# The factors of queries and keys in the second attention, as one power of minus a half on GpSimd

## The chip, the cores and the metric

The kernel runs on one core of a Trainium2 chip. The metric is the device time of one execution in microseconds (us); less is better.

## What is computed

Two transformer blocks in a row over 1024 positions of width 1024, in fp32. The change lies in the second block, in the preparation of queries and keys for its stick-breaking attention with eight heads of 64 columns:

```python
def rms_norm(x, g):
    return (x * lax.rsqrt(jnp.mean(x * x, axis=-1, keepdims=True) + EPS)) * g

q = rms_norm(q.reshape(bsz, s_len, ATTN_HEADS, HEAD_DIM), q_norm_g[i])
k = rms_norm(k.reshape(bsz, s_len, ATTN_HEADS, HEAD_DIM), k_norm_g[i])

def stick_breaking_attention(q, k, v):
    for qb in range(s_len // Q_BLOCK):
        z = einsum(qi, kj) * HEAD_DIM ** -0.5          # causal, s < t
        log_rem = where(causal, log_sigmoid(-z), 0.0)
        suffix = cumsum(log_rem, reverse=True) - log_rem
        weights = where(causal, exp(log_sigmoid(z) + suffix), 0.0)
        o = einsum(weights, vj)
```

The factor `rsqrt(mean + EPS)` of each head and position is what the change computes in another way.

## The kernel before

The program is written out engine by engine; each engine runs its own queue in the order of the code, and semaphores tie them. TensorE computes every projection as three matmuls for each tile of 128 rows (high part times high part, low part, and again), so each unit of weights (128x1024) has to be split into w_hi and w_lo. In the stretch of the change GpSimd does the splitting: `split` computes w_hi as w_raw plus a column of zeros and w_lo as w_raw minus w_hi, unit u starting when TensorE has finished both halves of unit u - 2.

The second attention works on pairs of heads; the code's `HEADS` is 4, and "head" below is such a pair, number p from 0 to 3. A head is cut into `NSEG` = 12 segments n: a block of 128 queries against up to 512 keys, 128, 256, 384 or 512 columns wide. Segments 0 to 4, 6, 8 and 10 end in the masked diagonal; 5, 7, 9 and 11 are the remaining 512 columns of the queries of the segment before. For each segment and each of the two heads in the pair (hh):

- TensorE: logits (line 1737) into a bank, and, one segment behind, the transposes of the weights (line 1747), then, two behind, the product with the values (line 1761). Between these, `norm_fill` and `fill` put matmuls of the projections that come next (lines 1199 to 1201; three units for a head: queries, keys, values).
- ScalarE (all its instructions have line 2829): `sb`, the sigmoid of minus z; `sa`, the sigmoid of z; `swt`, a copy of the transposed weights. In its queue of segment n the order is sb(n) twice, swt(n-1, 0), sa(n) twice, swt(n-1, 1).
- VectorE: `remains`, two scans (line 2681) over sb; `weights`, the mask on the diagonal (line 2692) and the product `sw` of sa and the scan (line 2697). At the end of a segment it moves finished projections out of their banks (line 1912).

While head p runs, the factors of head p + 1 are made. ScalarE squares its queries and keys (`square`), TensorE sums the squares (`head_sums`, line 1268) into a bank as a tile of 128x256, and then, on the tile hsm (128x256):

- VectorE, after the products of segment 6: `head_mean`, mean plus EPS, from the bank into hsm (line 1933), which raises `st_var`;
- ScalarE, after segment 7's queue: `head_sqrt`, the root in place, which raises `st_root`; the sigmoid and the root are in different tables, so a table load stands before and behind it;
- VectorE, after the products of segment 7: `head_factor`, the reciprocal in place (line 1938), which raises `st_inv`;
- SyncE's queue: `spread_qk_factors`, 16 rows of hsm to memory (line 970) and four transfers back that spread them over all partitions of `spread_qk` (line 976). Behind them in this queue stand the loads of the next units of weights (line 984);
- VectorE, at segment 10: scales queries and keys of the next head by the gain and by spread_qk (line 2731).

This happens for heads 1, 2 and 3 (`SPREAD_QK`). Head 0 uses the same functions through `head_inverse` and gets its factors by matmuls; so does a norm behind the attention.

Of the kernel before, what the change touches and what calls it, by code (L numbers as in the profile page):

```python
# [22 lines left out]
ALU = mybir.AluOpType  # L23
# [3 lines left out]
P = 128  # L27
T = 1024
# [6 lines left out]
HEADS = 4  # L35
# [18 lines left out]
DER = {}  # L54
_at = 0
for _name, _n in (("fin_n1", 8), ("subln", 1), ("qn", 1), ("neg_lam", 1), ("lb", 8), ("omlb", 8),
                  ("g0", 8), ("g1", 8), ("lamp", 2), ("lame", 2), ("zero", 1)):
    DER[_name] = _at
    _at += _n
NDER = _at  # L60
# [7 lines left out]
U_SB = U_PLE + KT  # L68
# [4 lines left out]
U_OUT2 = U_SU + 2  # L73
# [10 lines left out]
N_FIN = N_PLE + 1  # L84
N_1 = N_FIN + 1
N_QK = N_1 + 1
# [6 lines left out]


SPREAD_QK = tuple(range(N_QK + 1, N_QK + HEADS))


def bc_no(n):

    return n + 1 - len([m for m in SPREAD + SPREAD_QK if m <= n])  # L100

# [162 lines left out]
def half_no(u, hf):  # L264

    return 2 * u + hf + 1
# [35 lines left out]
def da_calm(u):  # L302
    h, n = divmod(u - U_DA - 6, 3)
    if h + 1 < HEADS:
        return KT * h + (3, 6, 8)[n], KT * h + (4, 7, 9)[n]
    return ((KT * h + 5, KT * h + 6), (KT * h + 8, KT * h + 8))[n]
# [45 lines left out]
S_SUM = 13  # L352


def bass_two_blocks(nc, io):
    ctx = ExitStack()
    with ctx:
        def at(name, cols, off, dt=F32, parts=P):
            shape = [parts, *cols] if isinstance(cols, tuple) else [parts, cols]
            return nc.alloc_sbuf_tensor_at(name, shape, dt, offset=SBUF_BASE + off)  # L360

        def sem(name):
            return ctx.enter_context(nc.semaphore(name))
# [24 lines left out]
        der = at("der", NDER, VEC_END)  # L388
# [85 lines left out]
        hsm = at("hsm", T // 4, S0 + 57 * KB)  # L474
# [113 lines left out]
        st_var = sem("st_var")  # L588
        st_root = sem("st_root")
        st_inv = sem("st_inv")  # L590
# [22 lines left out]
        der_ready = sem("der_ready")  # L613
# [378 lines left out]
        def _(pool):  # L992
            pool.memset(der[:, DER["zero"]:DER["zero"] + 1], 0.0).then_inc(der_ready, 1)
            pool.wait_ge(der_ready, 1)
            zero = der[:, DER["zero"]:DER["zero"] + 1]
            pool.memset(sinm[:, :], 0.0).then_inc(cs_clear, 1)
            pool.memset(cosm[:, :], 1.0).then_inc(cs_clear, 1)
            for m in range(2):
# [2 lines left out]
            def split(u0, n, cols=(T, T)):  # L1001
                def one_unit(u, s, turn, high_there, calm=None):
                    if not high_there:
                        if calm:
                            pool.wait_ge(w_ready, calm[0])
                        pool.wait_ge(w_in[s], 16 * (turn + 1))

                        pool.wait_ge(acc_full, half_no(u - 2, 1))
                        nc.gpsimd.tensor_tensor(w_hi[:, s, 0:cols[s]], w_raw[:, s, 0:cols[s]],  # L1009
                                                zero.to_broadcast([P, cols[s]]), ALU.add).then_inc(w_hi_done, 1)  # L1010
                    pool.wait_ge(w_hi_done, u + 1)
                    if calm:
                        pool.wait_ge(w_ready, calm[1])
                    nc.gpsimd.tensor_tensor(w_lo[:, s, 0:cols[s]], w_raw[:, s, 0:cols[s]],  # L1014
                                            w_hi[:, s, 0:cols[s]].bitcast(F32), ALU.subtract).then_inc(w_split, 1)

                if u0 == 0:
                    for s in range(2):
                        one_unit(s, s, 0, True)
                    with pool.Fori(1, n // 2, 1) as i:  # L1020
                        for s in range(2):
                            one_unit(2 * i + s, s, i, False)
                    for u in range(n, U_HG + 5):
                        one_unit(u, u % 2, u // 2, False, da_calm(u))
                else:
                    with pool.Fori(0, n // 2, 1) as i:
                        for s in range(2):
                            one_unit(u0 + 2 * i + s, s, u0 // 2 + i, False)
# [143 lines left out]
            split_ahead(U_SB + 2)  # L1172
            pool.wait_ge(st_inv, N_1 + 1)
            split_ahead(U_SB + 3)
            split(U_SB + 4, U_OUT2 - U_SB - 4)
            lows_and_sums(FF2, U_OUT2, T, Q_2)
            feed_forward(FF2, of2, U_PLE2)
            split(U_PLE2 + 2, KT - 2)
# [706 lines left out]
        def _(dve):  # L1885
# [5 lines left out]
            def step(ins):  # L1891

                ins.then_inc(dve_step, 1)
                steps[0] += 1
                dve.wait_ge(dve_step, steps[0])
# [38 lines left out]

            def head_factor(n):

                dve.wait_ge(st_root, n + 1)
                nc.vector.reciprocal(hsm[:, :], hsm[:, :]).then_inc(st_inv, 1)

            def head_inverse(n):  # L1940
# [3 lines left out]
            def row_inverse(n, scale):  # L1944

                dve.wait_ge(st_sum, n + 1)
                ts(rsm[:, :], ps[:, 7, 0:P], scale, EPS, ALU.mult, ALU.add).then_inc(st_var, 1)
                dve.wait_ge(st_root, n + 1)
                nc.vector.reciprocal(rsm[:, :], rsm[:, :]).then_inc(st_inv, 1)

            def da_guard(h):
# [224 lines left out]
            for h in range(HEADS):  # L2176
                u = U_HG + 5 * h
# [107 lines left out]
                for d in range(2):  # L2285

                    n = 2 * h + d
# [367 lines left out]
            dve.wait_ge(st_sum, N_1 + 1)  # L2655
            fin, both = hsm[:, 0:P], hsm[:, P:2 * P]
            ts(fin, ps[:, 7, 0:P], 1.0 / T, EPS, ALU.mult, ALU.add).then_inc(st_var, 1)
            dve.wait_ge(st_root, N_FIN + 1)
            nc.vector.reciprocal(fin, fin).then_inc(st_inv, 1)
            dve.wait_ge(st_inv, N_FIN + 1)  # L2660
            step(stt(both, ps[:, 7, P:2 * P], 1.0 / T, fin, ALU.mult, ALU.mult))
            step(tt(both, both, fin, ALU.mult))
            ts(both, both, EPS, None, ALU.add).then_inc(st_var, 1)
            dve.wait_ge(st_root, N_1 + 1)
            step(nc.vector.reciprocal(both, both))
            tt(both, both, fin, ALU.mult).then_inc(st_inv, 1)
            dve.wait_ge(rstd_ready, 4)
# [41 lines left out]
            for p in range(HEADS):  # L2709
                slots = sb_slots(p)  # L2710
                u_next = sb_fill(p)[0]
                if p + 1 < HEADS:
                    next_ = [sk[(p + 1) % 2][:, 0, :], sk[(p + 1) % 2][:, 1, :], sv[:, :]]
                else:
                    next_ = [cc[:, j, :] for j in range(3)]
                for n in range(NSEG + 1):
                    if n < NSEG:
                        remains(p, n, 0)
                        remains(p, n, 1)
                        weights(p, n, 0)  # L2720
                        weights(p, n, 1)
                    if p + 1 < HEADS:
                        if n == S_SUM // 2:
                            head_mean(N_QK + p + 1, 1)
                        elif n == S_SUM // 2 + 1:
                            head_factor(N_QK + p + 1)
                    evict(slots[2 * n] + slots[2 * n + 1], u_next, next_)
                    if p + 1 < HEADS and n == NSEG - 2:
                        dve.wait_ge(qk_fac_in, 64 * (p + 1))
                        for t, gain in enumerate((dcol("qn"), col("kn"))):  # L2730
                            stt(sk[(p + 1) % 2][:, t, :], sk[(p + 1) % 2][:, t, :], gain, spread_qk[:, t, :],
                                ALU.mult, ALU.mult).then_inc(qk2_ready, 1)
# [94 lines left out]
        def _(act):  # L2827
# [29 lines left out]
            def head_sqrt(n):  # L2857

                act.wait_ge(st_var, n + 1)
                av(hsm[:, :], hsm[:, :], ACT.Sqrt).then_inc(st_root, 1)  # L2860
# [146 lines left out]
            for h in range(HEADS):  # L3007
                u = U_HG + 5 * h
# [400 lines left out]
            for p in range(HEADS):  # L3409
                if p == 0:  # L3410
                    square(0, 0)
                    square(0, 1)
                    act.wait_ge(st_bc, bc_no(N_1))
                    av(rstd_f[:, :], banks(2), ACT.Copy).then_inc(xf_ready, 1)
                    head_sqrt(N_QK)
                    act.wait_ge(x_out, 16 * KT)
                for n in range(NSEG + 2):
                    if n < NSEG:
                        betas(p, n, 0, True)
                        betas(p, n, 1, True)  # L3420
                    if n == 6 and p + 1 < HEADS:
                        square(p + 1, 1)
                    if n == 0:
                        act.wait_ge(sv_tr, p + 1)
                        av(svt[:, :, :], banks(6).rearrange("p (c e) -> p c e", c=KT),
                           ACT.Copy).then_inc(sv_ready, 1)
                    if 1 <= n <= NSEG:
                        turned_weights(p, n - 1, 0)
                    if n < NSEG:
                        betas(p, n, 0, False)  # L3430
                        betas(p, n, 1, False)
                    if 1 <= n <= NSEG:
                        turned_weights(p, n - 1, 1)
                    if n >= 2:
                        out_rows(p, n - 2)
                    if p + 1 < HEADS:
                        if n == 4:
                            square(p + 1, 0)
                        elif n == 7:
                            head_sqrt(N_QK + p + 1)  # L3440


            act.wait_ge(so_out, 2 * HEADS)
# [164 lines left out]
```

## Time and profile before

| | us |
|---|---|
| median of 3 runs | 2714.21 |
| lowest, highest run | 2710.95, 2714.23 |
| the profiled execution | 2713.26 |
| its span | 2711.5 |

| engine | busy, us | share of the span |
|---|---|---|
| TensorE (PE) | 2653.9 | 98% |
| VectorE (DVE) | 1985.6 | 73% |
| GpSimd (POOL) | 1359.2 | 50% |
| ScalarE (ACT) | 1121.3 | 41% |

The granted clock of TensorE is 0.998 of full speed. Times in rows are microseconds from the start of the span. The second attention runs from about 1515 to 1795; the factors for head 1 are made between 1563 and 1585, those for heads 2 and 3 about 69 and 138 us later. In a timeline, x2 means two instructions in a row that were merged, and the bracket at the end tells how long the engine stood idle before the first and what released it. The ends of matmuls are modelled: one is shown with 0.39 us where the next starts 0.23 us later.

### The profile page before, as it was taken

What the parts mean: (1) busy time and instruction counts of PE and PEld (TensorE: products, weight loads), DVE (VectorE), ACT (ScalarE), POOL (GpSimd) and SP (SyncE); (2) the same over time, 40 slices, a digit from 0 to 9 for tenths busy, and PEclk for the clock granted to TensorE, in tenths of its full rate; (3) what the DMA queues carried; (4) which work ended last, traced back from release to release, by engine and by line L of the source; (5) the groups of instructions that cost most, each with busy time, mean ns of one, the idle gap of its engine ahead of it and who ended that gap; (6) DMA issues with size and microseconds to landing.
All of it is one profiled execution on the core that took longest, in us unless ns stands there. A gap on an engine that the chain in (4) does not pass through costs nothing. (4 is left out here: it accounts for less than half of the span.)

```text
span 2711.5 us, 37992 instructions
## 1 busy us (share of the span) xinstructions
PE 2653.9 (98%) x14526; PEld 2141.4 (79%) x14526; DVE 1985.6 (73%) x2333; ACT 1121.3 (41%) x1628; POOL 1359.2 (50%) x878
## 2 busy tenths in 40 slices
PE   8999999999999999999999999999999999999999
PEld 6888877777778888878888766678778888888877
DVE  8777676778877766687778687855776566877775
ACT  5555533342443333344453355532243334444451
POOL 3111100002477777788945322122567777888842
PEclk9999999999999999999999999999999999999999
DMA  3111111112123323444412111112223435544412
GB/s 126 36 44 28 40 47 40 40 32 102 44 78 112 109 82 113 144 164 155 158 49 100 49 40 40 40 38 72 76 96 143 163 139 201 175 156 148 151 59 77
DMA packets 103437, 251.31 MB, mean 93 GB/s; under 512 B 10872, under 2 KB 14816, under 8 KB 99808
## 3 DMA queue, kind: packets, MB, share of 16 engines
q1 hardware_dynamic: 98944, 234.88, 26.4%
q10 hardware_dynamic: 4320, 14.09, 1.3%
q8 instruction: 113, 1.85, 0.3%
q14 instruction: 60, 0.49, 0.1%
HBM read 188.46 MB, written 58.11 MB: 91 GB/s over the span
## 5 line engine op out<-in xcount | busy, mean ns | idle before, releaser
L1009 POOL TENSOR_TENSOR w_hi<-w_raw,der 128x1024 fp32r<-128x1024 f32 (+1 forms) x55 | 100.0, 1818 | 848.9 <-PE ps L1201 767.9
L1199 PE MATMUL ps<-a_hi,w_hi 128*128 128x512 f32 x1120 | 463.7, 414 | 11.4 <-POOL w_lo L1014 10.1
L1201 PE MATMUL ps<-a_hi,w_lo 128*128 128x512 f32 x1120 | 439.8, 393 | 0.0
L1200 PE MATMUL ps<-a_lo,w_hi 128*128 128x512 f32 x1120 | 438.7, 392 | 0.0
L1067 POOL TENSOR_TENSOR w_lo<-w_raw,w_hi 128x512 fp32r<-128x512 f32 x212 | 290.4, 1372 | 122.9 <-ACT w_hi L2829 122.7
L2829 ACT ACTIVATE w_hi<-w_raw 128x512 fp32r<-128x512 f32 (+1 forms) x249 | 169.3, 681 | 364.2 <-PE ps L1336 189.2
L2459 DVE TENSOR_TENSOR x<-ps,x 128x512 f32<-128x512 f32 x356 | 236.8, 688 | 32.2 <-PE ps L1382 32.2
L1199 PEld LDWEIGHTS ps<-a_hi,w_hi 128*128 128x128 f32 x1120 | 212.1, 189 | 57.9 <-issue 16.9
L1067 POOL TENSOR_TENSOR w_lo<-asum,w_hi 128x512 fp32r<-128x512 f32 x151 | 210.0, 1391 | 85.2 <-ACT w_hi L2829 85.2
L1201 PEld LDWEIGHTS ps<-a_hi,w_lo 128*128 128x128 f32 x1120 | 211.0, 188 | 46.4
L1200 PEld LDWEIGHTS ps<-a_lo,w_hi 128*128 128x128 f32 x1120 | 212.1, 189 | 35.3 <-issue 0.2
L2829 ACT ACTIVATE w_hi<-asum 128x512 fp32r<-128x512 f32 x151 | 95.4, 632 | 281.0 <-POOL asum L1114 103.7
L1014 POOL TENSOR_TENSOR w_lo<-w_raw,w_hi 128x1024 fp32r<-128x1024 f32 (+1 forms) x57 | 148.4, 2603 | 67.6 <-DVE de L2057 60.9
L1380 PE MATMUL ps<-fb_ring,w_hi 128*128 128x512 f32 x448 | 174.3, 389 | 0.0
L1381 PE MATMUL ps<-fb_ring,w_hi 128*128 128x512 f32 x448 | 174.3, 389 | 0.0
L1382 PE MATMUL ps<-fb_ring,w_lo 128*128 128x512 f32 x448 | 174.3, 389 | 0.0
L2535 DVE TENSOR_TENSOR uv<-ps,uv 128x512 f32<-128x512 f32 x36 | 24.9, 692 | 156.6 <-PE ps L1336 153.7
L1334 PE MATMUL ps<-fa_comb,w_hi 128*128 128x512 f32 x352 | 137.4, 390 | 0.6 <-DVE fa_comb L2362 0.6
L1335 PE MATMUL ps<-fa_comb,w_hi 128*128 128x512 f32 x352 | 137.0, 389 | 0.0
L1336 PE MATMUL ps<-fa_comb,w_lo 128*128 128x512 f32 x352 | 137.0, 389 | 0.0
L2468 DVE TENSOR_TENSOR fb_ring<-fb_wait,fb_ring 128x1024 fp32r<-128x1024 f32 x56 | 95.0, 1698 | 49.0 <-ACT fb_ring L2829 49.0
L1380 PE MATMUL ps<-fa_ring,w_hi 128*128 128x512 f32 x308 | 120.6, 392 | 1.9 <-DVE fa_ring L2468 1.9
(462 smaller groups left out, 6706.9 us busy)
## 6 DMA issues: line engine op xcount, KB each, us to landing
fb_wait<-hidden SPq DMA_DIRECT2D x56, 512.0 KB, 3.8
w_raw<-in_w_mix SPq DMA_DIRECT2D x54, 512.0 KB, 3.6
hidden<-hcomb SPq DMA_DIRECT2D x27, 1024.0 KB, 3.9
w_raw<-in_w_f SPq DMA_DIRECT2D x96, 256.0 KB, 3.2
w_raw<-in_w_gu SPq DMA_DIRECT2D x88, 256.0 KB, 2.6
fa_wait<-hidden SPq DMA_DIRECT2D x28, 512.0 KB, 3.8
hidden<-hbuf SPq DMA_DIRECT2D x27, 512.0 KB, 5.9
w_raw<-in_w_ple SPq DMA_DIRECT2D x16, 512.0 KB, 3.5
```

The source lines that it names most:

```text
L1014: nc.gpsimd.tensor_tensor(w_lo[:, s, 0:cols[s]], w_raw[:, s, 0:cols[s]], w_hi[:, s, 0:cols[s]].bitcast(F32), ALU.subtract).then_inc(w_spli ...
L1067: nc.gpsimd.tensor_tensor(ring(w_lo, r), src, ring(w_hi, r).bitcast(F32), ALU.subtract).then_inc(e_lo, 1)
L1199: mm(ps[:, bank, :], wh, hi[:, k, cols], start=(n == 0), stop=False)
L1200: mm(ps[:, bank, :], wh, lo[:, k, cols], start=False, stop=False)
L1201: last = mm(ps[:, bank, :], wl, hi[:, k, cols], start=False, stop=(n == nk - 1))
L1334: mm(ps[:, bank, :], wh, hi, start=start, stop=False, skip_group_check=True)
L1335: mm(ps[:, bank, :], wh, lo, start=False, stop=False, skip_group_check=True)
L1380: mm(out, wh, hi, start=(jj == 0 and at_ in (0, 1, 4, 5)), stop=False, skip_group_check=True)
L1381: mm(out, wh, lo, start=False, stop=False, skip_group_check=True)
L1382: last = mm(out, wl, hi, start=False, stop=(ends and at_ not in (0, 1, 4)), skip_group_check=True)
L2459: tt(dst, ps[:, ff.bank(g, at_, c), :], dst, ALU.add).then_inc(x_add, 1)
L2829: return nc.scalar.activation(out, in_, f, **kw)
```

## The change

The root on ScalarE and the reciprocal on VectorE for heads 1 to 3 go. In their place GpSimd raises hsm in place to the power of a new column `mhalf`, which holds -0.5 and is broadcast along the 256 columns; it waits for `st_var` and raises `st_inv`. To have a place for it in GpSimd's queue, the loop that split the units of the second block's projections is written out with `split_ahead`, and the power stands before the split of units U_SB + 7, U_SB + 10 and U_SB + 13. The other waits on `st_root` count three fewer where they come later (`root_no`). The column costs one more memset and one more wait at GpSimd's start.

```diff
+def root_no(n):
+
+    return n + 1 - len([m for m in SPREAD_QK if m <= n])
...
+            mhalf = der[:, DER["mhalf"]:DER["mhalf"] + 1]
+            pool.memset(mhalf, -0.5).then_inc(der_ready, 1)
+            pool.wait_ge(der_ready, 2)
...
             pool.wait_ge(st_inv, N_1 + 1)
             split_ahead(U_SB + 3)
-            split(U_SB + 4, U_OUT2 - U_SB - 4)
+            for u in range(U_SB + 4, U_OUT2):
+                p, t = divmod(u - U_SB - 7, 3)
+                if t == 0 and 0 <= p < HEADS - 1:
+                    pool.wait_ge(st_var, N_QK + p + 2)
+                    nc.gpsimd.tensor_tensor(hsm[:, :], hsm[:, :], mhalf.to_broadcast([P, T // 4]),
+                                            ALU.pow).then_inc(st_inv, 1)
+                split_ahead(u)
...
             def head_factor(n):
 
-                dve.wait_ge(st_root, n + 1)
+                dve.wait_ge(st_root, root_no(n))
                 nc.vector.reciprocal(hsm[:, :], hsm[:, :]).then_inc(st_inv, 1)
...
                     if p + 1 < HEADS:
                         if n == S_SUM // 2:
                             head_mean(N_QK + p + 1, 1)
-                        elif n == S_SUM // 2 + 1:
-                            head_factor(N_QK + p + 1)
...
                     if p + 1 < HEADS:
                         if n == 4:
                             square(p + 1, 0)
-                        elif n == 7:
-                            head_sqrt(N_QK + p + 1)
```

The order of the instructions around it, first on ScalarE in head 0, segments 6 to 8 (sb, sa and swt as above; line numbers of each kernel's own text). Before:

```order
L2829 ACTIVATE swt<-ps 128x256
L2829 ACT_TABLE_LOAD
L2829 ACTIVATE hsm<-hsm 128x256
L2829 ACT_TABLE_LOAD
L2829 ACTIVATE sb<-ps 128x384 x2
L2829 ACTIVATE swt<-ps 128x512
```

and now:

```order
L2841 ACTIVATE swt<-ps 128x512
L2841 ACTIVATE sb<-ps 128x512 x2
L2841 ACTIVATE swt<-ps 128x256
L2841 ACTIVATE sa<-ps 128x512 x2
L2841 ACTIVATE swt<-ps 128x256
L2841 ACTIVATE sb<-ps 128x384 x2
L2841 ACTIVATE swt<-ps 128x512
```

The root and its two table loads are gone from between swt of segment 6 and sb of segment 8; nothing else moved. VectorE at the same place, from the mean on (the scans print as SCALAR_TENSOR_TENSOR on srem). Before:

```order
L1933 TENSOR_SCALAR hsm<-ps 128x256
L2681 SCALAR_TENSOR_TENSOR srem<-sb,srem,past 128x512 x2
L2697 TENSOR_TENSOR sw<-sa,srem 128x512 x2
L1938 RECIPROCAL hsm<-hsm 128x256
L2681 SCALAR_TENSOR_TENSOR srem<-sb,past 128x384 x2
```

and now:

```order
L1947 TENSOR_SCALAR hsm<-ps 128x256
L2695 SCALAR_TENSOR_TENSOR srem<-sb,srem,past 128x512 x2
L2711 TENSOR_TENSOR sw<-sa,srem 128x512 x2
L2695 SCALAR_TENSOR_TENSOR srem<-sb,past 128x384 x2
L2706 TENSOR_TENSOR sa<-sa,ctri 128x128
```

The reciprocal is gone; the two scans of segment 7 stand right behind the mean, as before. GpSimd over the first units of the attention, now (before, the loop of lines 1008 to 1014 stood here with the same two instructions for each unit and nothing between):

```order
L1043 TENSOR_TENSOR w_hi<-w_raw,der 128x1024
L1046 TENSOR_TENSOR w_lo<-w_raw,w_hi 128x1024
L1187 TENSOR_TENSOR hsm<-hsm,der 128x256
L1043 TENSOR_TENSOR w_hi<-w_raw,der 128x1024
L1046 TENSOR_TENSOR w_lo<-w_raw,w_hi 128x1024
```

The power (line 1187) stands between the split of unit U_SB + 6 and that of U_SB + 7, and again three and six units later.

## Rows read from the trace of the kernel before

**Rows 1.** The page: busy time by engine, and the chain by engine.

```profile
PE 2653.9 (98%) x14526; PEld 2141.4 (79%) x14526; DVE 1985.6 (73%) x2333; ACT 1121.3 (41%) x1628; POOL 1359.2 (50%) x878
...
PE 31%; DVE 2%; issue 2%; POOL 1%; ACT 0%; DVEq 0%; POOLq 0%
```

**Rows 2.** Waits, 1565 to 1591: us in total, times, longest.

```profile
PE ps L1747 <- DVE sw L2697: 1.4, 1, 1.4
...
PE ps L1747 <- ACT swt L2829: 0.9, 1, 0.9
```

**Rows 3.** Timeline of ACT, 1567 to 1572: start, us, instruction.

```profile
1568.06 1.28 ACT L2829 ACT_TABLE_LOAD   x1
1569.35 0.42 ACT L2829 ACTIVATE hsm<-hsm 128x256 f32<-128x256 f32 x1
1569.78 1.28 ACT L2829 ACT_TABLE_LOAD   x1
```

**Rows 4.** Timeline of DVE, 1565 to 1590.

```profile
1565.47 0.42 DVE L1933 TENSOR_SCALAR hsm<-ps 128x256 f32<-128x256 f32 x1
1565.81 2.45 DVE L2681 TENSOR_TENSOR_SCAN srem<-sb,srem,past 128x512 f32<-128x512 f32 x2
1568.17 1.27 DVE L2697 TENSOR_TENSOR sw<-sa,srem 128x512 f32<-128x512 f32 x2
1569.80 1.75 DVE L1938 RECIPROCAL hsm<-hsm 128x256 f32<-128x256 f32 x1 [0.36 <-ACT hsm L2829]
...
1582.65 0.29 DVE L2692 TENSOR_TENSOR sa<-sa,ctri 128x128 f32<-128x128 f32 x1 [0.74 <-ACT sa L2829]
...
1584.51 1.28 DVE L2731 SCALAR_TENSOR_TENSOR sk_odd<-sk_odd,der,spread_qk 128x1024 f32<-128x1024 f32 x1
...
1586.90 2.46 DVE L2681 TENSOR_TENSOR_SCAN srem<-sb,srem,past 128x512 f32<-128x512 f32 x2
```

**Rows 5.** Timeline of PE, 1569 to 1590: transposes of weights.

```profile
1569.61 0.66 PE L1747 MATMUL ps<-ident,sw 128*128 128x128 f32 x4
...
1572.58 0.63 PE L1747 MATMUL ps<-ident,sw 128*128 128x128 f32 x4 [0.92 <-ACT swt L2829]
...
1590.00 0.66 PE L1747 MATMUL ps<-ident,sw 128*128 128x128 f32 x4 [1.42 <-DVE sw L2697]
```

**Rows 6.** Timeline of POOL in the attention.

```profile
1541.25 1.89 POOL L1009 TENSOR_TENSOR w_hi<-w_raw,der 128x1024 fp32r<-128x1024 f32 x1 [12.87 <-PE ps L1201]
1543.22 3.20 POOL L1014 TENSOR_TENSOR w_lo<-w_raw,w_hi 128x1024 fp32r<-128x1024 f32 x1
...
1561.06 2.65 POOL L1014 TENSOR_TENSOR w_lo<-w_raw,w_hi 128x1024 fp32r<-128x1024 f32 x1
1593.90 1.89 POOL L1009 TENSOR_TENSOR w_hi<-w_raw,der 128x1024 fp32r<-128x1024 f32 x1 [30.20 <-PE ps L1201]
...
1662.94 1.89 POOL L1009 TENSOR_TENSOR w_hi<-w_raw,der 128x1024 fp32r<-128x1024 f32 x1 [30.20 <-PE ps L1201]
```

**Rows 7.** DVE's scans: timeline, then the line's min/median/max ns, 1543.5 to 1545.

```profile
1541.81 5.69 DVE L2681 TENSOR_TENSOR_SCAN srem<-sb,past 128x512 f32<-128x512 f32 x2
...
L2681 DVE TENSOR_TENSOR_SCAN srem<-sb,past x2: 2412/2882/3352, 1541.8 to 1544.1; 128x512 f32<-128x512 f32 x2
```

**Rows 8.** Timeline of POOL: w_lo of 512 and of 1024 columns.

```profile
1302.09 1.29 POOL L1067 TENSOR_TENSOR w_lo<-w_raw,w_hi 128x512 fp32r<-128x512 f32 x1
...
1526.00 2.39 POOL L1014 TENSOR_TENSOR w_lo<-w_raw,w_hi 128x1024 fp32r<-128x1024 f32 x1
```

**Rows 9.** SyncE's queue, timeline; then the answer on line 976, landing.

```profile
1571.58 0.52 SPq L970 DMA_DIRECT2D qk_factors<-hsm  x1
1573.35 2.65 SPq L976 DMA_DIRECT2D spread_qk<-qk_factors  x4
...
DMA to landing us min/median/max: 3.9/4.8/6.0
```

**Rows 10.** Timeline of POOL at the start of the span.

```profile
7.50 5.75 POOL L1014 TENSOR_TENSOR w_lo<-w_raw,w_hi 128x1024 fp32r<-128x1024 f32 x2 [2.98 <-ACT w_hi L2829]
```

More of the change, by code:

```diff
@@ L56 @@
 for _name, _n in (("fin_n1", 8), ("subln", 1), ("qn", 1), ("neg_lam", 1), ("lb", 8), ("omlb", 8),
-                  ("g0", 8), ("g1", 8), ("lamp", 2), ("lame", 2), ("zero", 1)):
+                  ("g0", 8), ("g1", 8), ("lamp", 2), ("lame", 2), ("zero", 1), ("mhalf", 1)):
     DER[_name] = _at
@@ L1947, in row_inverse @@
                 ts(rsm[:, :], ps[:, 7, 0:P], scale, EPS, ALU.mult, ALU.add).then_inc(st_var, 1)
-                dve.wait_ge(st_root, n + 1)
+                dve.wait_ge(st_root, root_no(n))
                 nc.vector.reciprocal(rsm[:, :], rsm[:, :]).then_inc(st_inv, 1)
@@ L2657, in _ @@
             ts(fin, ps[:, 7, 0:P], 1.0 / T, EPS, ALU.mult, ALU.add).then_inc(st_var, 1)
-            dve.wait_ge(st_root, N_FIN + 1)
+            dve.wait_ge(st_root, root_no(N_FIN))
             nc.vector.reciprocal(fin, fin).then_inc(st_inv, 1)
@@ L2663, in _ @@
             ts(both, both, EPS, None, ALU.add).then_inc(st_var, 1)
-            dve.wait_ge(st_root, N_1 + 1)
+            dve.wait_ge(st_root, root_no(N_1))
             step(nc.vector.reciprocal(both, both))
```

## The prediction

> **What bounds the kernel now.** I read the page first: TensorE (PE) is busy 98% of a span of 2711.5 us, and the chain that ended last is named by its matmuls [rows 1]. So a microsecond taken from VectorE (DVE), ScalarE (ACT) or GpSimd (POOL) is worth something only where PE stands still for it. The change touches one place, met three times: heads 0, 1 and 2 of the second attention (56% to 64% of the span), each preparing the factors for the head after it. The three are alike: POOL's split after 30.20 us of waiting comes at 1593.90 and again at 1662.94, 69.04 us later [rows 6]. I therefore price one head and multiply by three.
>
> For that stretch I read who waited for whom [rows 2]: PE stands 0.9 us once for ACT's copy of turned weights (swt) and 1.4 us once for a DVE product (sw). Each is short; together they bound what a head can give at 2.3 us. ACT's timeline [rows 3] shows the first one's cause: its queue holds a table load, the root and a second table load (1.28 + 0.42 + 1.28, from 1568.06 to 1571.06) ahead of the sb and swt activations. DVE [rows 4] stands 0.36 us for the root, then spends 1.75 us on the reciprocal. PE [rows 5] turns the first half of segment 7 at 1569.61 without waiting, stops before 1572.58 (0.92), and again before 1590.00 (1.42).
>
> **What is removed.** Per head ACT loses 3.0 us and DVE 1.75 + 0.36 = 2.1 us. What PE gets back is less. With the tables gone, swt of segment 7 starts when its transposes end and PE's 0.92 us goes: the fills behind are PE's own work. What is late next is the 1.42 us stop before 1590.00, and I don't expect it to go. Its DVE product comes after two scans (2.46 us) and two scalings with the spread factors (2.4 us), ahead of these after segment 10's masks and products, and those began after DVE itself stood 0.74 us for ACT's sa [rows 4]. That sa is queued behind an swt that had waited for PE's transposes. So the loop PE, ACT, DVE, PE sets the time there: if PE comes 0.9 earlier, sa, product and the stop all move 0.9 and the stop keeps its length. The removal is worth 0.92 a head, 2.8 us in all, not 3 x 2.1.
>
> **What is added.** A power of 128x256 on POOL, issued when DVE's mean is done (1565.47 + 0.42 = 1565.9). POOL's queue is free: its split ends at 1563.7 and the next starts at 1593.90 [rows 6]. Anything under 28 us delays no split behind it.
>
> POOL's time is not the price, though; DVE's is. At 1541.81 two scans of 512 columns take 5.69 us [rows 7], where two take 2.46 elsewhere [rows 4]. POOL ran from 1541.25 to 1543.14 and from 1543.22 for 3.20 us [rows 6]. The first scan takes 2.41 us and ends at 1544.22: 1.08 after w_hi ended, so it moved nothing until then. The second takes 3.35 and ends about 1.1 after w_lo did. A DVE instruction with two SBUF inputs waits for the whole of a POOL instruction that reads SBUF, and POOL gets in between two scans. The Trainium skill says so too (SBUF — State Buffer, Who interferes with whom: a DVE instruction with two SBUF inputs contends with a GpSimd instruction that reads SBUF, and the lock is exclusive). The trace agrees for sums and differences, with 5.69 against 2.46; no row here shows it for a power.
>
> By order of the queues, DVE's next instruction after the mean is the scan of segment 7's first half. It is issued at 1565.81, runs to 1567.07, then the power (X us) goes in, and the second scan and both products start X later. The first product, before at 1568.17 + 0.69 = 1568.86, comes at 1568.86 + X; PE wants it at 1569.61, so about 0.7 us of X is covered by PE's own work. Beyond that PE stands, and the loop above hands the delay on undiminished. Per head: **-0.92 + (X - 0.7) = X - 1.6**; even at X = 1.6 us.
>
> **X.** No row of the trace is a power on POOL. From below: differences of 512 and 1024 columns take 1.29 and 2.39 us [rows 8], 2.15 ns a column and 0.19 fixed, so one pass over 256 columns is 0.74 us (0.55 without the fixed part). At that price the time falls by 3 x 0.9 = 2.6 us. Next up: DVE's reciprocal costs 1.75/0.42 = 4.2 times the simple instruction on the same tile [rows 4]; the same factor on 0.74 is 3.1 us, and 3 x 1.5 = +4.5 us. From above: a power worked out in software is a logarithm, a product and an exponential with their special cases; at some twenty passes of 0.55 it is 11 us, +28 us in all. I take X = 6 us, the geometric mean of 3.1 and 11: nearer to neither, because a program's loop won't be as cheap as one hardware divide and should do better than twenty passes through SBUF. By a page's figure alone (the Trainium skill, GPSIMD Engine Reference, section 3.1: data-dependent branching costs about 12 cycles an element, on top of about 2.6 for two inputs, at 1.2 GHz) an estimate would be 256 x 14.6 / 1.2 GHz = 3.1 us and a sum of +4.5; no run here shows that figure.
>
> **Smaller parts, at nothing.** The factors' way through memory: before, hsm is ready at 1571.55 and the last of four spreading transfers is issued at about 1575.4 and lands within 6.0 [rows 9], by 1581.4, 9.9 after; DVE wants them at 1584.51. Now they are ready at 1567.07 + X + 9.9 and wanted at 1584.51 + X - 1.6, nearly 6 us later at any X. SP's next weight load behind them is for a unit that POOL splits only 16 us after 1593.90. The new memset at the start moves POOL by a fraction of 1 us, ahead of 2.98 us of waiting for ACT [rows 10]. The unrolled splits are the same instructions, and they wait for PE.
>
> **The sum.** 3 x (6 - 1.6) = +13.2 us. The profiled execution is 2713.26 us around its span of 2711.5; the median of the runs shown is 2714.21. On the median that is 2727.4; I say **2727**. The measurement tells about 0.2% (5.4 us) from no change; that is crossed at X = 3.4 us.
>
> **Rivals.**
> (a) The power is slow and holds DVE off (forecast): X from 3.4 to 21 us, 2719.6 to 2772, likeliest 2727. For it: the blocked scans and the software nature of the work. Chance 0.50.
> (b) The power is cheap, X under 3.4 us: 2711.6 to 2719.6, at X = 2 about 2715.4. For it: POOL's loops in this trace run at 2.15 ns a column with no sign of a high fixed cost. Within 0.2%. Chance 0.22.
> (c) The power doesn't hold DVE's second input while it computes, because its reads come far apart. Then only the 0.92 is left, 2711.4, as long as the factors arrive (X under 7.6: 1565.9 + X + 9.9 against 1584.51 - 0.92). Against it: POOL's instructions in rows 7 held it to their end. Within 0.2%. Chance 0.10.
> (d) X beyond 21 us, a loop element by element: over 2772; past 28 us it also delays POOL's next split. Chance 0.11.
> (e) Faster: the lead of DVE reaches the product before 1590.00, so both stops go, 3 x (0.92 + 1.42) = 7.0 us, 2707. It needs X under about 1 us or case (c), and an sa that comes early by itself. Against it: DVE's 0.74 us wait for ACT. Chance 0.05.
> (f) The change does not take away what it says, for instance table loads return elsewhere in the head. In the order of the built program ACT has 9 rows fewer (three roots, six loads) and DVE three reciprocals fewer, so only an unseen replacement would do it; same time. Chance 0.02.
>
> Faster by over 0.2%: 0.05 (e). Within: 0.22 + 0.10 + 0.02 = 0.34. Slower: 0.50 + 0.11 = 0.61. The range runs from 2711, just under (b) and (c), to 2772, the end of (a); outside are (d) and (e), 0.16. It is wide because X is. The likeliest case's own range is 2719.6 to 2772.
>
> **What would show it.** In the profile after, ACT has no table load between sb activations in heads 0 to 2, and its sb of segment 8 follows swt at once; POOL has three instructions on hsm, whose length is X; one DVE scan of segment 7 grows from 1.25 to about 1.25 + X; PE stands before the first transposes of segment 7 for X - 0.7, named after the DVE product, and its 0.92 for swt is gone; the stop before 1590.00 keeps its 1.4. The heads are 69.04 + X - 1.6 apart. If DVE's scan keeps 1.25 us beside a long power, (a) is wrong and (c) right. If X is under 3 us, the price is wrong and the mechanism stands. If the 1.42 stop shrinks, my reading of the loop is wrong. If the heads are 69.04 apart with an early swt, PE had another limit there.

## The result

| | before | after |
|---|---|---|
| median, us | 2712.58 (4 runs) | 2815.36 (4 runs) |
| lowest, highest | 2710.49, 2714.23 | 2814.64, 2818.18 |
| the profiled execution, its span | 2713.26, 2711.5 | 2818.18, 2816.4 |

The ratio is 1.0383 with a 95% interval of 1.0371 to 1.0395: about 103 us slower. The forecast was slower, 2727, with a range that ended at 2772. One of the eleven executions of the version in "The same values in fewer columns" below took 3296.74 us at a granted clock of 0.753 and is in no ratio; without it the median of that version is 2711.4.

The page of the changed kernel shows where: TensorE's busy share and its granted clock have holes where they had none. The span is cut into forty equal slices; each digit is the busy share, or the clock, of one slice in tenths:

```profile
PE   8999999999999999999999594599999999999999
...
PEclk9999999999999999999999797799999999999999
```

The power itself comes first. This is the answer on its line in the changed kernel, min/median/max in ns, and under it TensorE's largest wait between 1500 and 1900 (us in total, times, longest) and VectorE's wait for the spread factors:

```profile
L1187 POOL TENSOR_TENSOR hsm<-hsm,der x3: 42033/42042/42042, 1566.8 to 1775.1; 128x256 f32<-128x256 f32 x3
...
PE ps L1761 <- DVE sw L2711: 107.8, 3, 36.3
...
DVE sk_odd L2743 <- DMA spread_qk<-qk_factors: 69.1, 2, 34.8
DVE sk_even L2743 <- DMA spread_qk<-qk_factors: 34.2, 1, 34.2
```

A power of 128x256 takes 42.04 us, seven times my 6. VectorE's timeline in head 0 answers to [rows 4] and [rows 7] (start, us, instruction, idle before it and its releaser):

```profile
1566.29 0.41 DVE L1947 TENSOR_SCALAR hsm<-ps 128x256 f32<-128x256 f32 x1
1566.63 2.76 DVE L2695 TENSOR_TENSOR_SCAN srem<-sb,srem,past 128x512 f32<-128x512 f32 x2
1569.32 1.26 DVE L2711 TENSOR_TENSOR sw<-sa,srem 128x512 f32<-128x512 f32 x2
...
1583.56 0.69 DVE L2711 TENSOR_TENSOR sw<-sa,srem 128x512 f32<-128x512 f32 x1
1618.58 1.28 DVE L2743 SCALAR_TENSOR_TENSOR sk_odd<-sk_odd,der,spread_qk 128x1024 f32<-128x1024 f32 x1 [34.33 <-DMA spread_qk<-qk_factors]
```

While the power runs from 1566.79 to 1608.83, the two scans take 2.76 us where they took 2.45, and everything after them its usual time. VectorE is not held off. It stops later, at 1584.25 (34.33 us before 1618.58), because the factors are not there. SyncE's queue shows their way, as in [rows 9], with the same lengths and 37 us later:

```profile
1608.86 0.52 SPq L975 DMA_DIRECT2D qk_factors<-hsm  x1
1610.63 2.65 SPq L981 DMA_DIRECT2D spread_qk<-qk_factors  x4
```

From the power's end to VectorE's start is 1618.58 - 1608.83 = 9.75 us. TensorE stands behind VectorE, and when it starts again its clock is low. In this table by stretches the columns behind the length are busy us of TensorE, its weight loads, VectorE, ScalarE and GpSimd, then the granted clock, the DMA share and GB/s:

```profile
1583.00:1588.00 5.00, 4.80 (x48) 3.46 (x46) 1.22 (x3) 3.30 (x7) 5.00 (x1) 1.00 0.00 0
1588.00:1620.00 32.00, 0.24 (x6) 0.00 (x1) 1.42 (x2) 0.00 (x0) 20.83 (x1) 0.53 0.19 50
...
1622.00:1626.00 4.00, 1.93 (x7) 1.64 (x8) 2.62 (x4) 0.60 (x1) 0.00 (x0) 0.50 0.00 0
1626.00:1630.00 4.00, 4.00 (x32) 2.78 (x31) 0.69 (x1) 0.60 (x1) 0.60 (x1) 0.79 0.00 0
...
1628.00:1630.00 2.00, 2.00 (x22) 1.31 (x19) 0.69 (x1) 0.00 (x0) 0.60 (x1) 1.00 0.00 0
...
1630.00:1635.00 5.00, 5.00 (x31) 4.11 (x28) 3.20 (x3) 2.48 (x8) 3.67 (x2) 1.00 0.09 10
```

The granted clock falls to half (1.2 of 2.4 GHz) in the wait and is whole again by 1628, so the first matmuls after the wait run slowly: 0.63 us as modelled, against 0.39. TensorE starts again at 1624.07; the 0.79 over 1626 to 1630 puts the end of the low clock at about 1627.7. By this estimate 3.6 us ran at half speed, which loses 1.8.

What was meant to be won is there too. ScalarE goes from swt to sb at once, where [rows 3] had 3.0 us of tables and root, and TensorE turns segment 7's second half at 1572.25 without a wait, where [rows 5] had 0.92:

```profile
1568.39 0.40 ACT L2841 ACTIVATE swt<-ps 128x256 f32<-128x256 f32 x1
1568.65 0.91 ACT L2841 ACTIVATE sb<-ps 128x384 f32<-128x384 f32 x2
...
1572.02 0.39 PE L1215 MATMUL ps<-a_hi,w_lo 128*128 128x512 f32 x1
1572.25 0.60 PE L1761 MATMUL ps<-ident,sw 128*128 128x128 f32 x4
```

The powers start 104.15 us apart (1566.8, 1775.1, half of the difference) where heads were 69.04 apart: 35.1 us more for each of three heads, 105.3 us, where the span grew by 104.9.

### The profile page after: what moved, and what is told of

It reads as the page before. It is cut to its first block and busy times, and to the rows that moved or that the text cites. A ratio compares the mean times of both kernels' runs of the same rounds, so it can differ in the third digit from the quotient of the medians.

```text
span 2816.4 us, 37938 instructions
## 1 busy us (share of the span) xinstructions
PE 2656.0 (94%) x14526; PEld 2144.0 (76%) x14526; DVE 1982.6 (70%) x2330; ACT 1112.1 (39%) x1619; POOL 1485.3 (53%) x882
## 5 line engine op out<-in xcount | busy, mean ns | idle before, releaser
L1017 POOL TENSOR_TENSOR w_hi<-w_raw,der 128x1024 fp32r<-128x1024 f32 (+1 forms) x37 | 65.8, 1778 | 586.4 <-PE ps L1215 505.5
L1043 POOL TENSOR_TENSOR w_hi<-w_raw,der 128x1024 fp32r<-128x1024 f32 x20 | 39.9, 1996 | 248.4 <-PE ps L1215 244.7
L1761 PE MATMUL ps<-ident,sw 128*128 128x128 f32 x288 | 52.9, 295 | 108.7 <-DVE sw L2711 107.8
L2841 ACT ACTIVATE swt<-ps 128x512 f32<-128x512 f32 (+3 forms) x96 | 47.4, 494 | 224.3 <-PE ps L1761 224.3
L1022 POOL TENSOR_TENSOR w_lo<-w_raw,w_hi 128x1024 fp32r<-128x1024 f32 (+1 forms) x39 | 100.5, 2576 | 65.6 <-DVE de L2071 60.5
```

What stands on the lines that cost most here:

```text
L2841: return nc.scalar.activation(out, in_, f, **kw)
```

## The experiments

After the result my theory was **late factors**: the power's only cost is that what it makes comes late, plus a clock that has fallen meanwhile. The rival was the prediction's own mechanism, **VectorE held off**, at X - 1.6 us a head for a power of X us. A third question was what X hangs on. "Heads apart" is half the distance between the first and the third power in a profile. Two times on different chips differ by 1 us or so; each verdict is against runs of the kernel before on the same chip.

### What the removal is worth

```diff
                     nc.gpsimd.tensor_tensor(hsm[:, :], hsm[:, :], mhalf.to_broadcast([P, T // 4]),
-                                            ALU.pow).then_inc(st_inv, 1)
+                                            ALU.add).then_inc(st_inv, 1)
```

> The power is replaced by an addition of the same two operands (128x256), so the factors are wrong; everything else is the changed kernel. It measures what the removal of the root, its table loads and the reciprocal is worth by itself, with a POOL instruction of 0.6 to 0.8 us in the power's place. Theory 'late factors' (the power's 42.04 us make the factors arrive late, nothing else costs): PE's stop for swt (0.92 us in each of three heads) is gone, the stop before DVE's product of segment 11 stays at 1.4: 2.6 to 3.3 us under the kernel before. Rival 'the written-out splits or the moved work cost something of their own': at or above the kernel before. Rival 'both stops go': 7 us under. The scan beside the addition should grow by up to 0.7 us if DVE waits for it.

Measured: 2709.38 against 2711.63, ratio 0.9990 (0.9981 to 0.9999), 2.3 us under. Heads are 68.0 apart: 1.04 us won in each, 3.1 in all. TensorE's stop for VectorE's product of segment 11 is there in full, 4.2 us in three heads. The addition's line and that wait, then VectorE's timeline in head 0:

```profile
L1187 POOL TENSOR_TENSOR hsm<-hsm,der x3: 1519/1520/1521, 1565.2 to 1701.2; 128x256 f32<-128x256 f32 x3
...
PE ps L1761 <- DVE sw L2711: 4.2, 3, 1.4
```

```profile
1564.74 0.42 DVE L1947 TENSOR_SCALAR hsm<-ps 128x256 f32<-128x256 f32 x1
1565.07 2.77 DVE L2695 TENSOR_TENSOR_SCAN srem<-sb,srem,past 128x512 f32<-128x512 f32 x2
```

So the loop was read rightly, and the written-out splits cost nothing that shows. The first scan has 1.11 us left when the addition's 1.52 us begin, and the addition ends 0.41 us after it: it waited for the scan that was running. Once it has begun, the addition costs the second scan 0.32 us, and the power of the same operands cost it 0.31. That is the first sign that what holds VectorE is not the length of the instruction.

### Fewer columns

Only the number of columns under the power changes; the diff is that of the version with 64.

```diff
-                    nc.gpsimd.tensor_tensor(hsm[:, :], hsm[:, :], mhalf.to_broadcast([P, T // 4]),
+                    nc.gpsimd.tensor_tensor(hsm[:, 0:64], hsm[:, 0:64], mhalf.to_broadcast([P, 64]),
                                             ALU.pow).then_inc(st_inv, 1)
```

> The power over 64 of the 256 columns; the other factors stay unrooted. If the time is proportional to columns it takes 10.5 us. Theory 'late factors': ready at mean + 10.5 + 9.75, which is about 2.8 us after DVE wants them, less 0 to 1.1 us of PE's earlier arrival: +1.7 to +2.8 us a head, 5 to 8.5 us over the kernel before. Rival of the prediction 'DVE is held off for the whole power': X - 1.6 = 8.9 a head, +27 us, and a scan of 12 us in the trace.

> The power over 128 columns: 21 us if proportional. Theory 'late factors': DVE waits 34.3 - 21 = 13.3 us for the spread factors in each head, +12.2 to 14 a head, +37 to +42 us in all, scans at 1.25 to 1.6 us. Rival 'DVE held off': 19.4 a head, +58 us, scan of 22 us. A fixed start-up cost of the power (code loading) would show as more than 21 us.

> The power over 32 of the 256 columns; the other factors stay unrooted. From 11.45 us for 64 columns and 21.64 for 128 (0.159 us a column, 1.25 fixed) it takes 6.35 us. Theory 'late factors': ready 6.35 + 9.8 to 10.3 = 16.2 to 16.7 us after the mean, wanted 17.5 after it, so nobody waits and the removal's 1.04 us a head is left: 3.1 us under the kernel before, 15 under the version with 64 columns. Rival of the prediction 'DVE held off': X - 1.6 = 4.8 a head, +14 us.

The other factors stay without their root. The power's line in the version with 64 columns, then with 128, then with 32:

```profile
L1187 POOL TENSOR_TENSOR hsm<-hsm,der x3: 11442/11447/11449, 1564.2 to 1711.9; 128x64 f32<-128x64 f32 x3
```

```profile
L1187 POOL TENSOR_TENSOR hsm<-hsm,der x3: 21633/21637/21642, 1564.9 to 1732.7; 128x128 f32<-128x128 f32 x3
```

```profile
L1187 POOL TENSOR_TENSOR hsm<-hsm,der x3: 6332/6337/6341, 1563.7 to 1699.6; 128x32 f32<-128x32 f32 x3
```

TensorE's wait for VectorE's product (us in total, times, longest) with 64 columns, where it has grown, and with 32, where it is that of the version with the addition:

```profile
PE ps L1761 <- DVE sw L2711: 17.6, 3, 6.4
...
PE ps L1761 <- DVE sw L2711: 4.2, 3, 1.4
```

| columns | power, us | wait for the factors, a head | heads apart | median (before on the same chip) |
|---|---|---|---|---|
| 32 | 6.34 | none | 67.95 | 2708.05 (2712.05), 0.9989 (0.9979 to 0.9998) |
| 64 | 11.45 | 4.4 | 73.85 | 2726.15 (2711.63), 1.0053 (1.0038 to 1.0069) |
| 128 | 21.64 | 13.8 | 83.9 | 2754.49, one run (2711.63) |
| 256 | 42.04 | 34.4 | 104.15 | 2815.36 (2712.58), 1.0383 |

The power grows by 0.159 us a column and has 1.25 fixed (what of that is its own is settled further down). Held off, VectorE would have cost 4.7, 9.9 and 20.0 us a head at 32, 64 and 128 columns; the heads grew by -1.1, 4.8 and 14.9. The version with 32 columns decides it: a power of 6.34 us in the very place costs nothing. The version with 64 was 6 to 9.5 us slower than I expected. Its 4.4 us wait is 1.6 over my 2.8: the power had the fixed part that I had left out (0.95), and the spreading took longer (10.3 us from the power's end to VectorE's start in head 0, not 9.75). The rest, 4.8 - (4.4 - 1.04) = 1.5 us a head, is what is left for the clock, which no run parts from the wait at 64 columns. (The two heads between the first and the third power waited 4.1 us on average; with these it is 1.7.) VectorE's start after its wait in head 0, then the table by stretches:

```profile
1585.97 1.28 DVE L2743 SCALAR_TENSOR_TENSOR sk_odd<-sk_odd,der,spread_qk 128x1024 f32<-128x1024 f32 x1 [4.30 <-DMA spread_qk<-qk_factors]
```

```profile
1585.00:1590.00 5.00, 0.66 (x13) 0.42 (x8) 4.03 (x4) 0.00 (x0) 0.00 (x0) 0.80 0.24 83
1590.00:1595.00 5.00, 3.54 (x15) 2.77 (x17) 2.01 (x3) 0.85 (x2) 0.00 (x0) 0.52 0.00 0
1595.00:1600.00 5.00, 5.00 (x40) 3.65 (x37) 2.30 (x3) 1.28 (x4) 3.25 (x2) 1.00 0.02 3
```

### A long power beside the old path

The root and the reciprocal stay where they were, and GpSimd does a power that nobody waits for.

```diff
-    return n + 1 - len([m for m in SPREAD_QK if m <= n])
+    return n + 1
...
                     pool.wait_ge(st_var, N_QK + p + 2)
-                    nc.gpsimd.tensor_tensor(hsm[:, :], hsm[:, :], mhalf.to_broadcast([P, T // 4]),
-                                            ALU.pow).then_inc(st_inv, 1)
+                    pool.wait_ge(der_ready, 2 + p)
+                    nc.gpsimd.tensor_tensor(guard[:, :], guard[:, :], mhalf.to_broadcast([P, P]),
+                                            ALU.pow).then_inc(der_ready, 1)
...
+                        elif n == S_SUM // 2 + 1:
+                            head_factor(N_QK + p + 1)
...
+                        elif n == 7:
+                            head_sqrt(N_QK + p + 1)
```

> The path of the kernel before (root on ScalarE, reciprocal on VectorE) with the written-out splits, and beside it a power over 128 columns of a tile that nobody reads, issued at the same place in POOL's queue and ended before the next split is due (21 us in a gap of 28). Theory 'late factors': nobody waits for it, so the time is that of the kernel before within 2 us. Rival 'a power in progress holds off DVE's instructions with two SBUF inputs': DVE loses about 20 us a head, +55 to +60 us.

Measured: 2712.17 against 2711.63, ratio 1.0003 (0.9994 to 1.0012). The power ran 21.64 us in each head, and the instructions with two inputs in SBUF beside it kept their times, but for 0.10 us of the first two scans. The power's line, and VectorE's timeline under it:

```profile
L1188 POOL TENSOR_TENSOR guard<-guard,der x3: 21633/21637/21643, 1565.0 to 1703.1; 128x128 f32<-128x128 f32 x3
```

```profile
1564.84 2.55 DVE L2696 TENSOR_TENSOR_SCAN srem<-sb,srem,past 128x512 f32<-128x512 f32 x2
1567.32 1.26 DVE L2712 TENSOR_TENSOR sw<-sa,srem 128x512 f32<-128x512 f32 x2
...
1574.47 2.45 DVE L2696 TENSOR_TENSOR_SCAN srem<-sb,srem,past 128x512 f32<-128x512 f32 x2
```

This shows directly that a power in progress doesn't hold VectorE off; the 128 columns cost the scans 0.10 us, the 256 of the changed kernel 0.31, and 64 or 32 nothing that shows.

### What the power's time hangs on

Three versions: 16 rows of 256 columns in place of 128 rows, one row, and all rows with the exponent 1.0. The diff is that of the version with 16 rows.

```diff
-                    nc.gpsimd.tensor_tensor(hsm[:, :], hsm[:, :], mhalf.to_broadcast([P, T // 4]),
+                    nc.gpsimd.tensor_tensor(hsm[0:16, :], hsm[0:16, :], mhalf[0:16, :].to_broadcast([16, T // 4]),
```

> The power over 16 of the 128 rows, all 256 columns; the other rows stay unrooted. If eight cores work side by side on 16 rows each, 16 rows take as long as 128: 42.0 us and the time of the changed kernel, +103 us. If the work is shared over all rows, it takes about 42/8 = 5.3 us, and the time falls to 3 us under the kernel before.

> The power over 1 row of 256 columns; the other rows stay unrooted. 16 rows took 42.03 us, as 128 did. If each core goes through the elements of its 16 rows one by one, one row takes 1.25 + 40.8/16 = 3.8 us and the time falls to 3 us under the kernel before. If it takes a column of 16 rows in one step whatever their number, it stays at 42 us and at the time of the changed kernel.

> The exponent column holds 1.0 in place of -0.5, so the factors are not the right ones. If the power's time depends on its values (a short way out for whole exponents), it falls under 42 us; if every element goes the same way, it stays at 42.0 us and the time at that of the changed kernel.

The power's line with 16 rows (busy us, mean ns, idle before), then with one row (min/median/max ns):

```profile
L1187 POOL TENSOR_TENSOR hsm<-hsm,der 16x256 f32<-16x256 f32 x3 | 126.1, 42034 | 6.8 <-DVE hsm L1947 6.8
```

```profile
L1187 POOL TENSOR_TENSOR hsm<-hsm,der x3: 42028/42035/42037, 1563.4 to 1771.8; 1x256 f32<-1x256 f32 x3
```

The powers took 42.03 us with 16 rows, 42.03 with one and 42.04 with the exponent 1.0 (2818.56, 2814.32 and 2817.97 us, single runs). The number of rows and this other exponent don't matter; columns do.

### The same values in fewer columns

Only 16 of hsm's 128 rows are read when the factors are spread. SyncE copies these to 128 rows of 32 columns of an unused tile, and the power runs on that. This version computes everything.

```diff
+                sp_.wait_ge(st_var, N_QK + p + 1)
+                sp_.dma_start(rsm[:, 0:32], hsm[0:P:8, :].rearrange("j (k c) -> j k c", k=8)).then_inc(qk_fac_out, 16)
                 sp_.wait_ge(st_inv, N_QK + p + 1)
-                sp_.dma_start(qk_factors[p - 1].rearrange("r g c -> (r g) c"), hsm[0:P:8, :]).then_inc(qk_fac_out, 16)
-                sp_.wait_ge(qk_fac_out, 16 * p)
+                sp_.dma_start(qk_factors[p - 1].rearrange("r g (k c) -> (r g k) c", k=8), rsm[:, 0:32]).then_inc(qk_fac_out, 16)
+                sp_.wait_ge(qk_fac_out, 32 * p)
...
-                    pool.wait_ge(st_var, N_QK + p + 2)
-                    nc.gpsimd.tensor_tensor(hsm[:, :], hsm[:, :], mhalf.to_broadcast([P, T // 4]),
+                    pool.wait_ge(qk_fac_out, 32 * p + 16)
+                    nc.gpsimd.tensor_tensor(rsm[:, 0:32], rsm[:, 0:32], mhalf.to_broadcast([P, 32]),
                                             ALU.pow).then_inc(st_inv, 1)
```

> Computes the whole output. Only 16 of the 128 rows of hsm are ever read. SyncE copies them as 128 rows of 32 columns into an unused tile, the power runs on 128x32, and the result goes to memory from there. The power should take 6.35 us as in the version with 32 columns; the copy adds 2 to 2.5 us before it. Ready 18.2 to 19 us after the mean, wanted 17.5 after: a wait of 0.7 to 1.5 us against 1.04 gained: -1 to +1.5 us in all, about 100 us under the changed kernel. If the time of the power hung on the number of useful values and not on the columns of each row, it would stay at 42 us.

Measured: 2711.84 against 2712.05, ratio 0.9996 (0.9986 to 1.0005): no difference from the kernel before, and about 103 us under the changed one. In head 0, the power, the two scans beside it and VectorE's start:

```profile
1567.49 5.65 POOL L1189 TENSOR_TENSOR rsm<-rsm,der 128x32 f32<-128x32 f32 x1 [4.13 <-DMA rsm<-hsm]
...
1565.47 2.46 DVE L2697 TENSOR_TENSOR_SCAN srem<-sb,srem,past 128x512 f32<-128x512 f32 x2
...
1583.44 1.28 DVE L2745 SCALAR_TENSOR_TENSOR sk_odd<-sk_odd,der,spread_qk 128x1024 f32<-128x1024 f32 x1 [0.34 <-DMA spread_qk<-qk_factors]
```

The factors come 0.3 us late. The power takes 5.65 here, 0.7 less than before on 32 columns, because less of a scan is left when it starts: 0.43 us of the second one, where there 1.11 us of the first were left. From the end of the running scan both take 5.22 us. So the power waits for that scan, and of the 1.25 fixed only about 0.1 is its own (5.22 - 32 x 0.159). The profile's heads are 68.15 apart, 0.9 us less than in the kernel before, but the runs don't tell 2.7 us from nothing here.

### The clock

The transposes at which TensorE stands get matmuls in front of them that fill the wait; their result is overwritten. The first version had 140 of them, the second 157.

```diff
                     for hh in range(2):
+                        if n == NSEG and hh == 0 and more:
+                            pe.wait_ge(swt_ready, 2 * (NSEG * p + n - 1))
+                            for _ in range(140):
+                                mm(ps[:, 6, :], a_hi[:, 0, 0:P], a_hi[:, 0, 0:HALF], start=True, stop=True)
                         if n <= NSEG:
                             turn(p, n - 1, hh)
```

> The changed kernel with 140 matmuls of 512 columns (31.7 us at full clock) into the transposes' bank in each of the three heads, before the transposes at which PE stood 34 to 36 us; their result is overwritten. They fill a wait and add no work to the path. If the low clock after the wait costs 1.85 us a head (35.11 us between heads, less 34.3 of waiting, plus the 1.04 gained), the granted clock stays at 1.0 and the time falls by about 5.5 us, to 2810. If the clock costs nothing, the time stays; if the matmuls outlast the wait, it rises.

This one missed, as no time was won: 2820.01 us, ratio 1.0397 (1.0379 to 1.0414). Its matmuls ended at 1620.5, 4.7 us before the transposes, and the clock fell in that gap all the same. The transposes with their wait, then the stretch around them:

```profile
1625.27 1.12 PE L1761 MATMUL ps<-ident,sw 128*128 128x128 f32 x4 [4.73 <-DVE sw L2715]
```

```profile
1620.00:1630.00 10.00, 5.27 (x22) 3.46 (x20) 5.81 (x6) 1.19 (x2) 0.00 (x0) 0.73 0.00 0
```

> As the run before with 157 matmuls in place of 140 in each head (0.229 us each, 35.9 us), because 140 ended 4.7 us before the transposes could start and the granted clock fell in that gap. Now the gap should be about 1 us. If the low clock costs 1.85 us a head, the granted clock stays at 1.0, the powers are 102.3 us apart instead of 104.15, and the time is 5.5 us under the changed kernel on the same chip. If the clock costs nothing, it is the same.

> The changed kernel unchanged, on the chip of the run beside it, as its reference: 103 us over the kernel before, powers 104.1 to 104.2 us apart.

The changed kernel on this chip: 2816.39 us, ratio 1.0383 (1.0365 to 1.0400), powers 104.55 apart. With 157 matmuls: 2812.44 us, ratio 1.0373 (1.0356 to 1.0390), powers 102.2 apart, and the clock stays whole:

```profile
1620.00:1630.00 10.00, 9.92 (x66) 7.40 (x65) 4.91 (x7) 3.44 (x9) 4.29 (x2) 1.00 0.02 3
```

The medians differ by 4.0 us, the profiles' spans by 6.4 (2816.4 and 2810.0), and three times the difference of the powers' distance is 7. Three of the four runs of the changed kernel lie above the slowest run with 157 matmuls, but the intervals of the two ratios overlap. So the clock's share is 4 to 7 us of the 103 as a best reading, and the runs alone hardly part it from nothing.

## Why the prediction was wrong

**The mechanism of the price (wrong).** The step that failed is "POOL's time is not the price, though; DVE's is", and with it X - 1.6 a head. It rested on [rows 6] and [rows 7], where scans stood until w_hi and w_lo had ended. I read that as "for the whole of a POOL instruction that reads SBUF". The rows could not tell the length of the instruction from the number of columns it reads, as both grew together. The power parts them: 256 columns cost VectorE 0.31 us whether GpSimd adds them (0.32) or spends 42 us on them, and 21.64 us beside the old path cost nothing. With X = 42.04 in it, my sum would have said +121 us, against 103 measured. The Trainium skill (SBUF — State Buffer, Who interferes with whom) lets a two-input instruction contend with a GpSimd instruction that reads SBUF; the contention is there, but a hold that lasts for the whole instruction is not what these runs show. My sentence that no row shows it for a power named the gap, and I gave it a chance of 0.10 only.

**X (wrong by seven times).** 42.04 us against 6. My upper estimate, twenty passes of 0.55 us, was 11. The slope is 0.159 us a column where a difference has 0.00215: about 74 passes. With no row of a power the bound from above was a guess at the number of passes, and it cut the range at 21 us. Case (d), X beyond 21, had 0.11. Each of the two failures was a rival; it took both.

**The factors' way through memory (right numbers, wrong conclusion).** I held it at nothing "at any X", because a VectorE held off would have wanted the factors later too. That hung on the first step. Case (c) had the sum that came true, used past its bound (which I gave as 7.6 us; its own terms make 7.8): 1565.9 + 42.04 + 9.9 - (1584.51 - 0.92) = 34.2 us of waiting a head, less 0.92, times 3 is 100 us. The runs give 34.4 - 1.04 + 1.7 = 35.1 a head, 105 us of span; the 1.7 is what is left for the clock.

**What the removal is worth (right).** Predicted 0.92 us a head, measured 1.04 with the addition. The stop of 1.42 stayed, as the loop through ScalarE's sa said it would, so two table loads, a root and a reciprocal, 4.7 us of engine time in a head, are worth 1 us.

**POOL's own queue (right in kind).** I said that under 28 us nothing behind the power is late. At 42 us the splits still wait for TensorE (20.57 us before the next one, against 30.20 in [rows 6]), since TensorE had stopped for the factors first.

**The clock (missed).** I had no term for it. By what is left over, a head loses 1.5 to 2.1 us to it once there is a wait, whether of 4.4 or of 34 us; with the wait of the changed kernel filled, the powers stood 2.35 us closer (102.2 for 104.55).

**The sign** was right, and the chance of slower was 0.61, but most of it stood on the wrong mechanism.

## What to carry to other kernels

Before work moves to an idle engine, find the time from its input to the first reader of its result, here 17.5 us from the mean to VectorE's scaling with about 10 of them spent in transfers, and compare the new instruction with what is left, not with the engine's idle gap of 28 us. If no trace shows the operation, run it alone on a few columns first: one run with 32 and one with 64 columns would have given its time, its slope and the point from which it costs anything. When two engines get in each other's way, look whether the hold follows the columns read or the instruction's length before using it as a price.

## What the runs showed of the hardware

- GpSimd's power of two fp32 tensors took 0.159 us a column and about 0.1 us fixed, counted from the end of the scan that was running when it started; 256 columns took the same on 1, 16 and 128 rows and with the exponent -0.5 or 1.0. So 4096 values in 32 columns took 5.65 us, and the same values among 256 columns 42.04.
- Beside a scan with two SBUF inputs, a power cost VectorE 0.31 us at 256 columns, 0.10 at 128 and nothing visible at 64 and 32, while it ran for 6 to 42 us. An addition of 256 columns cost it 0.32.
- A power or an addition on GpSimd that started beside a running scan with two SBUF inputs did its work only behind it: the power on 32 columns ended 5.22 us after the scan, whether 1.11 or 0.43 us of the scan had been left.
- TensorE's granted clock fell to half in a wait of 6 us as in one of 36, and in the 4.7 us behind the 140 matmuls. In the version with 64 columns it was 0.52 over 1590 to 1595, right when the work came back, and whole from 1595.
